# Three of eight convolution tiles on ScalarE and GpSimd with logarithms between filler copies, and the modulation's products on VectorE in the feed-forward

## The chip, the core and the metric

The kernel runs on one NeuronCore of a Trainium2 chip. TensorE (PE) multiplies, VectorE (DVE), ScalarE (ACT) and GpSimd (POOL) work on tiles of 128 partitions, and SyncE (SP) issues the loads of the weights. The metric is the device time of one execution in microseconds; a kernel's time is the median of its runs. All arithmetic is float32.

## The reference, cut to what matters

The whole is a transformer block (two attention mixers, cross-attention to a memory, a feed-forward with a squared ReLU), followed by a second block whose input is modulated by a condition. Three parts of it are touched.

```python
# modulation: a vector times w_ada (1024 x 6144), for the condition c and for c_ctx
mx = silu(c) @ w_ada + b_ada ; mc = silu(c_ctx) @ w_ada + b_ada
xsh1, xsc1, xg1, xsh2, xsc2, xg2 = split(mx, 6)     # only the first two are used of mc
px = (x * (1 + xsc1) + xsh1) @ w_in                 # ctx likewise, with mc
...
# feed-forward of the first block, ahead of it
x = x + square(relu(h @ w_ff_in)) @ w_ff_out        # 1024 -> 4096 -> 1024
...
# convolution branch of the second block, 1024 channels = 8 tiles of 128
u = a * sigmoid(g)                                  # conv_glu, 512 tokens
conv[t] = conv_b + sum_j dw[j] * u[t + j - 15]      # 31 taps for each channel
...
# the decays of the recurrent branch (HGRN), forward and backward
log_f = log(sigmoid(z))  ;  b = cumsum(log_f)       # b and its edges give the weights of keys
```

## The kernel before, in words

The kernel is one program for each engine; semaphores order them (`line.at(name)` is the count at which a named step is done). A generator such as `fill` or `Beside.steps` hands out a program's pieces a few at a time, so that a side job is written between the steps of the main one. The order of the code is the order on the engine. Weights come in panels of 2 MB, through three slots of SBUF in the order of the list `ORDER`: SyncE loads a panel when the panel three places before it has been released (`done`).

The stages in order of time are: norm and projection; the latent stage (`latent_*`), in which VectorE makes rotated queries and keys for four tiles of 128 tokens, `ro(i)`, and TensorE turns them, `T(i)`; the compression (`compress_*`, lines 555 to 672); the first attention; cross-attention; the feed-forward (`ffn_*`); HGRN for the first half of the heads (`hgrn_*` with gq 0), then for the second (gq 1); the merge of the branches; the second attention; and a mixture of experts, half of the span.

**Modulation.** `ada_tensor` (line 437) multiplies the pair of conditions (`SC`, 128 x 2 in each of eight pieces) by twelve panels `w_ada`: eight matmuls of 512 columns for each panel. ScalarE copies each row out (line 467); for panels 0 to 3 TensorE turns the row into columns for `MOD`, for 4 to 11 ScalarE sends it to memory (`ROWD`, semaphores `s_row`). These pieces stand between the steps of the latent stage and of the compression: panels 0 to 7 in the latent stage, 8 ahead of the key matmuls of the compression (line 642), 9 to 11 behind its value matmuls (line 650). The first attention waits for all rows, since the row buffer `RB` lies in its memory. `MOD` is first read in the feed-forward's last part (`modulated_*`).

**Feed-forward.** Eight panels `w_ff_in` give 32 tiles `h`: TensorE multiplies (line 258), ScalarE takes the ReLU (line 1338), VectorE squares (line 1354). Eight panels `w_ff_out` (line 1327) follow.

**HGRN, gq 1.** TensorE makes the projections q (4 tiles), z and zc for two directions (4 and 4 each) and v (6 tiles), all through eight banks of PSUM, and then two panels of filler work, 16 steps of `aside_tensor` (line 1385): projections that later stages need, which go through banks 6 and 7, a copy by ScalarE (line 1399) and a store by GpSimd (line 1409). ScalarE takes sigmoids and copies of the projections. Beside that, VectorE makes the convolution (`taps_vector`): for each of eight tiles k it multiplies the gated input, then does one product with a first tap (line 1467) and 30 of `sum = u * tap + sum` (line 1471) in SBUF. GpSimd loads the tiles (lines 1482, 1483) and stores the sums to memory (line 1487). The logarithms' buffers (`LOGS`) share memory with the tap tiles. So ScalarE first finishes its eight filler copies (`fill(16)`), waits for VectorE's last tap and for the stores (`s_cv`), and then runs the four logarithm jobs (`log_scalar`: absolute value, exponential, logarithm; lines 1500, 1502, 1504); VectorE turns each into cumulative sums (`log_vector`, lines 1515 to 1529), takes the differences to the edges (`decay`, line 1756), ScalarE exponentiates (lines 1685, 1686), VectorE weighs the keys (line 1760), and TensorE, which has been through its filler, turns them (line 1596's loop with its transposes, `kt`) and makes the states.

## Time and profile before

| | us |
|---|---|
| median of 3 runs | 4361.85 |
| lowest and highest of them | 4344.37 and 4363.55 |
| the profiled execution | 4348.94 |
| its span, first to last instruction | 4347.0 |

Busy shares of the span are 83% for TensorE, 50% for VectorE, 19% for ScalarE and 28% for GpSimd. A matmul in float32 is two records; 128 x 512 records follow each other at 0.43 us at the full clock. The rows below are one kind each: a timeline row is the start in us, the length of a run of like instructions, engine, line, operation, output and input, count, and in brackets how long the engine had been idle before and what released it. Times on GpSimd are rough.

### The profile page before, as it was taken

Reading aid. Unit: us, or ns where it says so; the run is one execution under the profiler, and the core shown is the slowest. Engines: PE = TensorE matmul, PEld = TensorE weight load, DVE = VectorE, ACT = ScalarE, POOL = GpSimd, SP = SyncE. Lnnn points to the kernel's source line nnn. Section 1 sums busy time; section 2 is a strip of 40 time slices with the busy share of each in tenths; the row PEclk is TensorE's granted clock in tenths of the full one; section 3 lists DMA queues with packets and bytes.
Section 4 is the critical chain, followed back from the end, with each engine's and each line's share of the span. In section 5 each row is a group of like instructions: output and inputs, shape, how many; then the busy total and the mean of one; then the engine's idle time right before and its main releaser. Section 6 shows DMA issues by size and latency. Waiting matters only on the chain.

```text
span 4347.0 us, 33067 instructions
## 1 busy us (share of the span) xinstructions
PE 3596.0 (83%) x10942; PEld 1813.3 (42%) x10942; DVE 2153.0 (50%) x4711; ACT 845.3 (19%) x1796; POOL 1226.4 (28%) x1151
## 2 busy tenths in 40 slices
PE   8778998999997989939999974668776877776877
PEld 4334554444453564426644563334232333232322
DVE  0547523100013567966525448863686876433442
ACT  1224422000032221132211223011121221111111
POOL 0200000000000000000001013453787777777774
PEclk9876999999999989969999987889898998988988
DMA  3340021222211112200222256774999999999996
GB/s 152 138 150 1 1 97 49 77 77 77 97 58 49 63 54 104 76 34 34 75 76 97 104 196 214 258 248 160 385 338 348 342 365 359 355 370 369 353 377 263
DMA packets 171912, 765.16 MB, mean 176 GB/s; under 512 B 19256, under 2 KB 19256, under 8 KB 160224
## 3 DMA queue, kind: packets, MB, share of 16 engines
q0 software_dynamic: 157904, 580.06, 36.2%
q1 hardware_dynamic: 13824, 182.97, 11.5%
q8 instruction: 89, 1.46, 0.1%
q14 instruction: 79, 0.65, 0.0%
q10 hardware_dynamic: 16, 0.02, 0.0%
HBM read 744.08 MB, written 18.89 MB: 176 GB/s over the span
## 4 chain that ended last, share of the span: by engine, by line
PE 49%; DVE 20%; issue 8%; DMA 5%; POOL 4%; ACT 2%; another core or an unknown queue 1%; POOLq 0%; DVEq 0%; ACTq 0%
PE ps L252 13%; PE ps L258 9%; PE ps L2591 8%; DVE arena L2668 5%; PE ps L1327 5%; PE ps L1385 5%; DVE arena L1471 4%; POOL arena L2638 4%; DMA arena<-in_pu,arena 3%; PE ps L1609 2%; PE ps L220 2%; DMA arena<-in_pv,arena 2%; PE ps L1596 1%; PE ps L831 1%
## 5 line engine op out<-in xcount | busy, mean ns | idle before, releaser
L2591 PE MATMUL ps<-arena 128*128 128x512 f32 x2048 | 1031.1, 655 | 385.0 <-issue 163.9
L2591 PEld LDWEIGHTS ps<-arena 128*128 128x128 f32 x2048 | 404.9, 206 | 991.1 <-issue 786.8
L2668 DVE CUSTOM_DVE_ANT_0 arena<-arena 128x1024 f32<-128x1024 f32 x512 | 622.5, 1221 | 387.8 <-DMA arena<-in_pu,arena 350.2
L252 PE MATMUL ps<-arena 128*128 128x512 f32 (+1 forms) x1768 | 755.0, 587 | 31.5 <-ACT arena L2157 24.4
L2638 POOL DMA_INDIRECT arena<-in_pu,arena x512 | 559.2, 1092 | 419.8 <-issue 96.5
L2638 POOL DMA_INDIRECT arena<-in_pv,arena x512 | 557.5, 1089 | 196.3 <-issue 136.0
L258 PE MATMUL ps<-arena 128*128 128x512 f32 (+2 forms) x1408 | 527.7, 536 | 3.1 <-DVE arena L1300 0.9
L252 PEld LDWEIGHTS ps<-arena 128*128 128x128 f32 x1768 | 337.2, 192 | 434.8 <-issue 429.7
L258 PEld LDWEIGHTS ps<-arena 128*128 128x128 f32 x1408 | 268.2, 191 | 262.8 <-issue 220.4
L220 PE MATMUL ps<-arena 128*128 128x128 f32 (+1 forms) x1062 | 191.4, 314 | 203.0 <-ACT arena L1686 59.8
L263 POOL TENSOR_TENSOR arena<-arena 128x1 f32<-128x1 f32 (+7 forms) x38 | 61.4, 1617 | 1012.6 <-DVE arena L675 427.7
L2607 ACT ACTIVATE arena<-arena 128x128 f32<-128x128 f32 x512 | 191.5, 396 | 760.2 <-PE ps L2591 345.4
L1385 PE MATMUL ps<-arena 128*128 128x512 f32 x640 | 293.0, 605 | 16.6 <-ACT arena L1686 12.8
L220 PEld LDWEIGHTS ps<-arena 128*128 128x128 f32 (+1 forms) x1062 | 138.4, 159 | 291.3 <-issue 100.6
L1327 PE MATMUL ps<-arena 128*128 128x512 f32 x512 | 220.2, 592 | 1.4 <-DVE arena L1354 1.4
L1409 POOL DMA_DIRECT2D aside<-arena x20 | 10.7, 534 | 710.8 <-ACT arena L1399 710.8
L1471 DVE SCALAR_TENSOR_TENSOR arena<-arena 128x512 f32<-128x512 f32 x240 | 180.6, 753 | 8.4
L1385 PEld LDWEIGHTS ps<-arena 128*128 128x128 f32 x640 | 118.6, 193 | 143.7 <-issue 125.5
L1327 PEld LDWEIGHTS ps<-arena 128*128 128x128 f32 x512 | 97.1, 190 | 123.7 <-issue 121.5
L1609 PEld LDWEIGHTS ps<-arena 128*128 128x128 f32 x896 | 119.0, 209 | 31.1 <-issue 17.4
L1283 POOL DMA_DIRECT2D x_spill<-arena x1 | 0.6, 578 | 447.6 <-DVE arena L1351 447.6
L1609 PE MATMUL ps<-arena 128*128 128x64 f32 x896 | 118.2, 289 | 6.2 <-DVE arena L1804 6.1
(334 smaller groups left out, 3120.8 us busy)
## 6 DMA issues: line engine op xcount, KB each, us to landing
arena<-in_w_in SPq DMA_DIRECT2D x27, 2048.0 KB, 9.6
arena<-in_w_ada SPq DMA_DIRECT2D x12, 2048.0 KB, 8.1
arena<-in_w_ff_in SPq DMA_DIRECT2D x8, 2048.0 KB, 7.8
arena<-in_w_ff_out SPq DMA_DIRECT2D x8, 2048.0 KB, 8.1
arena<-in_w_pq SPq DMA_DIRECT2D x8, 2048.0 KB, 8.1
aside<-arena POOLq DMA_DIRECT2D x20, 512.0 KB, 6.8
arena<-in_w_at SPq DMA_DIRECT2D x4, 2048.0 KB, 8.4
arena<-in_w_o SPq DMA_DIRECT2D x4, 2048.0 KB, 8.0
```

The lines of the kernel that those rows point to most:

```text
L220: return t.transpose(ps, src, ID[0:src.shape[0], 0:src.shape[0]])
L252: x = t.matmul(PS[:, b, 0:n], hT[:, k, i * 128:(i + 1) * 128], w[:, k, :], start=k == 0, stop=k == nk - 1)
L258: x = t.matmul(PS[:, b, 0:n], w[:, k, f * 128:(f + 1) * 128], hT[:, k, 0:n], start=k == 0, stop=k == nk - 1)
L263: return g.tensor_tensor(o, o, MH[0:o.shape[0], 0:o.shape[-1]], ALU.pow)
L1327: x = t.matmul(PS[:, 4 * c + i, :], AT[:, 8 * kk + k, 128 * i:128 * i + 128], w[:, k, :], start=kk == 0 and k == 0, stop=kk == 3 and k == 7)
L1385: x = t.matmul(PS[:, b, :], l, r, start=k == 0, stop=k == 7)
L1471: tap.V.own(v).scalar_tensor_tensor(out=cv, in0=u[:, j:j + 512], scalar=dw[:, 8 * j + k:8 * j + k + 1], in1=cv, op0=ALU.mult, op1=ALU.add) ...
L1609: x = t.matmul(PS[:, b, 64 * c:64 * c + 64].rearrange("p (n t) -> p n t", t=w), WL[lv % 4][:, o:o + 128], sides(WL[lv % 4][:, o:o + 128], ...
L2591: x = t.matmul(PS[:, b + c, :], DG[n % 4], row(f)[:, 512 * c:512 * c + 512], start=j == 0, stop=j == 127)
L2607: a.activation(DG[n % 4], ID, ACT.Copy, scale=GS[i][:, j:j + 1]).then_inc(*pe.A.step("dg", n))
L2638: g.indirect_dma_start(PLACES[SPOT[n]], None, d[tab], bass.IndirectOffsetOnAxis(ap=EXU[i][:, j:j + 1], axis=0)).then_inc(s_row_in[SPOT[n]] ...
L2668: v.tensor_tensor_reduce(row(f), row(f), TT[i], 1.0, 0.0, ALU.mult, ALU.add, DOT[i % 2][:, j:j + 1]).then_inc(*pe.V.step("dot", 128 * i + j))
```

## The change

Three things move.

- The `w_ada` panels leave the latent stage and the compression. They now stand in `ORDER` between the panels of the feed-forward, one behind each of the first twelve. For each, VectorE multiplies the eight 512-wide pieces by a column of `SC` and adds them up (two conditions for panels 0 to 3, one for 4 to 11); TensorE adds over the partitions, with 8 small matmuls against a column of ones for panels 0 to 3 and one 512-wide matmul for 4 to 11; ScalarE copies out. The attention no longer waits for `s_row`.
- The convolution of gq 1 is split. VectorE has tiles 0 to 4 and keeps the sums in PSUM (banks 4 and 5, which leaves six for the projections); ScalarE copies each sum out (`move_out`). For tiles 5 to 7 ScalarE makes each product into one of three buffers, and GpSimd adds it to the sum: 93 products, 90 adds.
- The four logarithm jobs stand between the 16 filler steps on ScalarE, where they stood behind all of them.

```diff
-        ORDER = ([("w_in", c) for c in range(4)] + [("w_ada", c) for c in range(9)] + [("w_cmp", 0), ("w_cmp", 1)]
-                 + [("w_ada", c) for c in range(9, 12)] + [("scratch", 0), ("w_xk", 0), ("w_xv", 0), ("w_out", 0), ("w_out", 1),
-                                                           ("w_xq", 0), ("w_xo", 0)]
-                 + [("w_ff_in", c) for c in range(8)] + [("w_ff_out", c) for c in range(8)]
+        FF = [("w_ff_in", c) for c in range(8)] + [("w_ff_out", c) for c in range(8)]
+        ORDER = ([("w_in", c) for c in range(4)] + [("w_cmp", 0), ("w_cmp", 1), ("scratch", 0), ("w_xk", 0), ("w_xv", 0),
+                                                    ("w_out", 0), ("w_out", 1), ("w_xq", 0), ("w_xo", 0)]
+                 + [p for c in range(12) for p in (FF[c], ("w_ada", c))] + FF[12:]
...
+        def ada_sums_tensor(t, c, banks):
+            t.wait_ge(*ad.V.at("acc", c))
+            b = bank(t, banks, ad.A, "row", c)
+            if c < 4:
+                for r in range(2):
+                    for k in range(4):
+                        x = t.matmul(PS[:, b, 8 * r + 2 * k:8 * r + 2 * k + 2], ADA[c % 2][r][:, 128 * k:128 * k + 128], cs("one")[:, 0:2],
+                                     start=True, stop=True)
+            else:
+                x = t.matmul(PS[0:2, b, :], cs("one")[:, 0:2], ADA[c % 2][0], start=True, stop=True)
+            x.then_inc(*ad.P.step("row", c))
+
...
+        def ada_sums_vector(v, c):
+            w = w3("w_ada", c)
+            v.wait_ge(*loaded("w_ada", c))
+            if c > 1:
+                v.wait_ge(*ad.P.at("row", c - 2))
+            for k in range(8):
+                ad.V.own(v)
+                for r in range(ada_conditions(c)):
+                    o, s = ADA[c % 2][r], SC[:, k, r:r + 1]
+                    if k == 0:
+                        v.tensor_scalar(o, w[:, k, :], s, None, ALU.mult).then_inc(*ad.V.step("acc", c))
+                    else:
+                        v.scalar_tensor_tensor(out=o, in0=w[:, k, :], scalar=s, in1=o, op0=ALU.mult, op1=ALU.add
+                                               ).then_inc(*ad.V.step("acc", c))
+            done("w_ada", c, ad.V)
...
                     mm_feat(t, b, HT, 8, w3("w_ff_in", c), a, 512).then_inc(*ff.P.step("h", 4 * c + a))
+                    if c and a == 1:
+                        ada_sums_tensor(t, c - 1, BANKS)
...
+                        if c == 0 and i == 1:
+                            ada_sums_tensor(t, 7 + kk, (4, 5, 6, 7))
+                        if c == 0 and kk == 3 and i == 3:
+                            ada_sums_tensor(t, 11, (4, 5, 6, 7))
...
                 v.tensor_tensor(AT[:, f, :], AT[:, f, :], AT[:, f, :], ALU.mult).then_inc(*ff.V.step("h", f))
+                if f % 4 == 0:
+                    ada_sums_vector(v, f // 4)
+            for c in range(8, 12):
+                ada_sums_vector(v, c)
+            ad.V.own(v)
...
+        s_cv = [sem(f"s_cv{k}") for k in range(8)]
+        s_tap = [sem(f"s_tap{k}") for k in range(5)]
+        TAPU = [A[:, TFo + 1054 * j:TFo + 1054 * j + 542] for j in range(5)]
+        TAPC = [A[:, TFo + 1054 * j + 542:TFo + 1054 * j + 1054] for j in range(5)]
+        TAPP = [A[:, TFo + 5270 + 512 * j:TFo + 5782 + 512 * j] for j in range(3)]
+        ONV, ONG = (0, 1, 2, 3, 4), (5, 6, 7)
+        TAPBANK = (4, 5)
...
+            def move_out(k):
+                a.wait_ge(*tap.V.at("conv", k))
+                a.activation(TAPC[tap_slot(k)], PS[:, TAPBANK[k % 2], :], ACT.Copy).then_inc(*tap.A.step("out", k))
+            for k in (0, 5, 1, 6, 2):
+                gate(k)
+                yield
+            for n, k in enumerate(ONG):
+                u, cv = TAPU[tap_slot(k)], TAPC[tap_slot(k)]
+                a.wait_ge(*tap.V.at("input", k))
+                for j in range(31):
+                    x = u[:, j:j + 512]
+                    if j == 0:
+                        a.activation(cv, x, ACT.Identity, scale=tap_weight(k, 0), bias=pr("cb")[:, k:k + 1]).then_inc(*tap.A.step("product", k, 0))
+                    else:
+                        m = 30 * n + j - 1
+                        if m > 2:
+                            a.wait_ge(*tap.G.at("sum", m - 3))
+                        a.activation(TAPP[m % 3], x, ACT.Copy, scale=tap_weight(k, j)).then_inc(*tap.A.step("product", k, j))
+                    yield
+                    if (n, j) == (0, 20):
+                        move_out(0)
+                    if (n, j) == (1, 7):
+                        move_out(1)
+                    if (n, j) == (1, 14):
+                        gate(3)
+                    if (n, j) == (1, 20):
+                        gate(7)
+                    if (n, j) == (1, 24):
+                        move_out(2)
+                    if (n, j) == (1, 28):
+                        gate(4)
+                    if (n, j) == (2, 11):
+                        move_out(3)
+            move_out(4)
 
         def taps_vector(v):
-            dw = pr("dw")
-            for k in range(8):
-                u, cv = TAPU[k % 6], TAPC[k % 6]
-                if k < 6:
+            def prepare(k, first):
+                u = TAPU[tap_slot(k)]
...
-                v.tensor_tensor(u[:, 15:527], u[:, 15:527], cv, ALU.mult).then_inc(*tap.V.step())
-                tap.V.own(v).tensor_scalar(cv, u[:, 0:512], dw[:, k:k + 1], pr("cb")[:, k:k + 1], ALU.mult, ALU.add
+                v.tensor_tensor(u[:, 15:527], u[:, 15:527], TAPC[tap_slot(k)], ALU.mult).then_inc(*tap.V.step("input", k))
+            for k in ONV:
+                u, sums = TAPU[tap_slot(k)], PS[:, TAPBANK[k % 2], :]
+                prepare(k, k < 3)
+                if k > 1:
+                    v.wait_ge(*tap.A.at("out", k - 2))
+                tap.V.own(v).tensor_scalar(sums, u[:, 0:512], tap_weight(k, 0), pr("cb")[:, k:k + 1], ALU.mult, ALU.add
                                            ).then_inc(*tap.V.step())
                 yield
+                if k in (0, 1, 3):
+                    prepare({0: 5, 1: 6, 3: 7}[k], k < 2)
                 for j in range(1, 31):
-                    tap.V.own(v).scalar_tensor_tensor(out=cv, in0=u[:, j:j + 512], scalar=dw[:, 8 * j + k:8 * j + k + 1], in1=cv,
+                    tap.V.own(v).scalar_tensor_tensor(out=sums, in0=u[:, j:j + 512], scalar=tap_weight(k, j), in1=sums,
                                                       op0=ALU.mult, op1=ALU.add).then_inc(*tap.V.step("conv", k))
                     yield
...
+            def add(n, k, first, last):
+                cv = TAPC[tap_slot(k)]
+                for j in range(first, last):
+                    g.wait_ge(*tap.A.at("product", k, j))
+                    tap.G.own(g).tensor_tensor(cv, cv, TAPP[(30 * n + j - 1) % 3], ALU.add).then_inc(*tap.G.step("sum", 30 * n + j - 1))
+            for k in (0, 5, 1, 6, 2):
+                fetch(k)
+            add(0, 5, 1, 26)
+            g.wait_ge(*tap.A.at("out", 0))
+            put(0)
+            add(0, 5, 26, 31)
+            g.wait_ge(*tap.G.at("sum", 29))
+            put(5)
+            g.wait_ge(s_cv[0], 16)
+            fetch(3)
+            add(1, 6, 1, 8)
+            g.wait_ge(s_cv[5], 16)
+            fetch(7)
+            add(1, 6, 8, 10)
+            g.wait_ge(*tap.A.at("out", 1))
+            put(1)
+            add(1, 6, 10, 18)
+            g.wait_ge(s_cv[1], 16)
+            fetch(4)
+            add(1, 6, 18, 31)
+            g.wait_ge(*tap.G.at("sum", 59))
+            put(6)
+            add(2, 7, 1, 8)
+            g.wait_ge(*tap.A.at("out", 2))
+            put(2)
+            add(2, 7, 8, 16)
+            g.wait_ge(*tap.A.at("out", 3))
+            put(3)
+            add(2, 7, 16, 31)
+            g.wait_ge(*tap.G.at("sum", 89))
+            put(7)
+            g.wait_ge(*tap.A.at("out", 4))
+            put(4)
 
...
+            banks = (0, 1, 2, 3, 6, 7) if gq else BANKS
             t.wait_ge(*loaded("w_in2", gq))
             for f in range(4):
-                b = bank(t, BANKS, st.V, "q", f)
+                b = bank(t, banks, st.V, "q", f)
...
             if gq:
                 fill(16)
+                t.wait_ge(*tap.A.at("out", 4))
```

In `hgrn_scalar`, with the number of side steps for gq 1 behind each q, z, zc and v tile going from 10, 11, 6 and 10 to 6, 6, 3 and 6, the end of the projections is now as follows. `taps_over` waits for VectorE's last tap and for all eight stores; TensorE waits for `move_out(4)` behind its filler.

```diff
+            if gq:
+                beside.work += [taps_over(a)] + [log_scalar(a, st, r) for r in range(4)]
+                for _ in range(16):
+                    fill(1)
+                    beside.steps(6)
             beside.steps(ALLSTEPS)
-            if gq:
-                fill(16)
-                a.wait_ge(*tap.V.end())
-                a.wait_ge(s_cv[0], 16)
-                a.wait_ge(s_cv[1], 16)
-                a.wait_ge(s_cv[2], 96)
-                beside.work += [log_scalar(a, st, r) for r in range(4)]
-                beside.steps(ALLSTEPS)
```

TensorE in the latent stage and the compression, before: L444 is a modulation panel, L252 the projections, L220 transposes, L642 and L650 keys and values, L919 the first scores of the attention.

```order
L220 MATMUL ps<-arena 128x128 x18
L252 MATMUL ps<-arena 128x512 x4
L252 MATMUL ps<-arena 128x128
L444 MATMUL ps<-arena 2x512 x32
L220 MATMUL ps<-arena 128x128 x36
L444 MATMUL ps<-arena 2x512 x8
L642 MATMUL ps<-arena 32x128 x32
L650 MATMUL ps<-arena 128x128 x32
L444 MATMUL ps<-arena 2x512 x24
L220 MATMUL ps<-arena 128x32 x2
L919 MATMUL ps<-arena 128x32 x8
```

After (lines 600, 608 and 874 are the old 642, 650 and 919):

```order
L220 MATMUL ps<-arena 128x128 x18
L252 MATMUL ps<-arena 128x512 x4
L252 MATMUL ps<-arena 128x128
L220 MATMUL ps<-arena 128x128 x36
L600 MATMUL ps<-arena 32x128 x32
L608 MATMUL ps<-arena 128x128 x32
L220 MATMUL ps<-arena 128x32 x2
L874 MATMUL ps<-arena 128x32 x8
```

No panel stands between the transposes any more, none behind the value matmuls. ScalarE in gq 1, from the last v copy to the first exponentials of the decays, before (L1671 v, L1399 filler copies, L1500 to L1504 logarithms):

```order
L1671 ACTIVATE arena<-ps 128x512
L1399 ACTIVATE arena<-ps 128x512 x8
L1500 ACTIVATE arena<-arena 128x1024
L1502 ACT_TABLE_LOAD
L1502 ACTIVATE arena<-arena 128x1024
L1504 ACT_TABLE_LOAD
L1504 ACTIVATE arena<-arena 128x1024
L1500 ACTIVATE arena<-arena 128x2048
L1502 ACT_TABLE_LOAD
L1502 ACTIVATE arena<-arena 128x2048
L1504 ACT_TABLE_LOAD
```

After (L1780 v, L1491 `move_out`, L1420 filler copies, L1601 to L1605 logarithms):

```order
L1491 ACTIVATE arena<-ps 128x512
L1780 ACTIVATE arena<-ps 128x512 x5
L1601 ACTIVATE arena<-arena 128x1024
L1603 ACT_TABLE_LOAD
L1603 ACTIVATE arena<-arena 128x1024
L1605 ACT_TABLE_LOAD
L1605 ACTIVATE arena<-arena 128x1024
L1420 ACTIVATE arena<-ps 128x512
L1601 ACTIVATE arena<-arena 128x2048
L1603 ACT_TABLE_LOAD
L1603 ACTIVATE arena<-arena 128x2048
L1605 ACT_TABLE_LOAD
```

The first logarithm job now stands ahead of all filler copies, the second behind one of them, and the last `move_out` ahead of five of the six v copies. ScalarE beside the z tiles of gq 1, before (L1664 and L1665 are z's sigmoid and copy, L1454 a gate):

```order
L1664 ACTIVATE arena<-ps 128x512
L1665 ACTIVATE arena<-ps 128x512
L1664 ACTIVATE arena<-ps 128x512
L1665 ACTIVATE arena<-ps 128x512
L1454 ACTIVATE arena<-arena 128x512
L1664 ACTIVATE arena<-ps 128x512
```

After (L1773, L1774 z, L1506 products for GpSimd, L1491 `move_out(2)`, L1487 gate):

```order
L1773 ACTIVATE arena<-ps 128x512
L1774 ACTIVATE arena<-ps 128x512
L1506 ACTIVATE arena<-arena 128x512
L1491 ACTIVATE arena<-ps 128x512
L1506 ACTIVATE arena<-arena 128x512 x4
L1487 ACTIVATE arena<-arena 128x512
L1506 ACTIVATE arena<-arena 128x512
L1773 ACTIVATE arena<-ps 128x512
L1774 ACTIVATE arena<-ps 128x512
L1506 ACTIVATE arena<-arena 128x512
```

Each copy of a z tile, which frees TensorE's bank, now has up to six products ahead of it, each product from the fourth on waiting for a GpSimd add.

## Rows read from the trace of the kernel before

**Rows 1.** The page, section 4: the chain that ended last, by engine.

```profile
PE 49%; DVE 20%; issue 8%; DMA 5%; POOL 4%; ACT 2%; another core or an unknown queue 1%; POOLq 0%; DVEq 0%; ACTq 0%
```

**Rows 2.** Timeline of TensorE, HGRN gq 1.

```profile
1652.07 110.27 PE L258 MATMUL ps<-arena 128*128 128x512 f32 x320 [0.73 <-DVE arena L245]
1762.17 41.36 PE L252 MATMUL ps<-arena 128*128 128x512 f32 x96
1803.37 55.10 PE L1385 MATMUL ps<-arena 128*128 128x512 f32 x128
1918.31 0.66 PE L220 MATMUL ps<-arena 128*128 128x128 f32 x2 [59.84 <-ACT arena L1686]
```

**Rows 3.** Timeline of VectorE, the same stage: one tile of taps, first and last of the logarithms.

```profile
1786.43 0.67 DVE L1466 TENSOR_TENSOR arena<-arena 128x512 f32<-128x512 f32 x1
...
1787.72 23.59 DVE L1471 SCALAR_TENSOR_TENSOR arena<-arena 128x512 f32<-128x512 f32 x30
...
1876.63 1.23 DVE L1515 SCALAR_TENSOR_TENSOR arena<-arena 128x1024 f32<-128x1024 f32 x1 [15.65 <-ACT arena L1504]
...
1911.84 2.29 DVE L1529 TENSOR_TENSOR arena<-arena 128x2048 f32<-128x2048 f32 x1
```

**Rows 4.** Timeline of ScalarE, the same stage.

```profile
1840.89 0.60 ACT L1399 ACTIVATE arena<-ps 128x512 f32<-128x512 f32 x1 [9.26 <-DMA aside<-arena]
...
1870.81 1.06 ACT L1500 ACTIVATE arena<-arena 128x1024 f32<-128x1024 f32 x1 [11.71 <-DMA conv<-arena]
...
1896.87 1.91 ACT L1504 ACTIVATE arena<-arena 128x2048 f32<-128x2048 f32 x1
...
1915.64 0.21 ACT L1685 ACTIVATE arena<-arena 128x8 f32<-128x8 f32 x1 [15.56 <-DVE arena L1756]
...
1926.55 0.36 ACT L1693 ACTIVATE arena<-ps 128x256 f32<-128x256 f32 x1
```

**Rows 5.** GpSimd's groups with shapes kept apart: busy, mean ns of one.

```profile
L263 POOL TENSOR_TENSOR arena<-arena 128x30 f32<-128x30 f32 x4 | 24.5, 6122 | 59.1 <-DVE arena L560 43.4 <-DVE arena L549 15.7
...
L1487 POOL DMA_DIRECT2D conv<-arena x8 | 4.3, 544 | 119.7 <-DVE arena L1464 119.5 <-DVE arena L1471 0.3
...
L378 POOL CAST lmask<-arena 128x1920 uint8<-128x1920 f32 x1 | 1.8, 1784 | 44.9 <-DMA arena<-in_lm 44.9
```

**Rows 6.** Timeline of VectorE, latent stage and compression.

```profile
174.36 2.16 DVE L547 TENSOR_TENSOR arena<-arena 128x1920 f32<-128x1920 f32 x1 [13.79 <-ACT arena L523]
...
199.75 2.16 DVE L547 TENSOR_TENSOR arena<-arena 128x1920 f32<-128x1920 f32 x1 [9.05 <-ACT arena L523]
...
227.74 0.96 DVE L576 TENSOR_TENSOR arena<-arena 128x768 f32<-128x768 f32 x1 [5.28 <-PE ps L220]
...
240.00 0.97 DVE L598 TENSOR_TENSOR arena<-arena 128x496 f32<-128x496 f32 x1
...
258.97 1.98 DVE L610 COPY arena<-ps 32x64 f32<-32x64 f32 x8 [14.03 <-PE ps L650]
...
286.11 0.49 DVE L987 TENSOR_TENSOR arena<-ps,arena 128x128 f32<-128x128 f32 x2 [21.42 <-DMA ada_rows<-arena]
```

**Rows 7.** Timeline of TensorE, latent stage and compression.

```profile
197.95 27.63 PE L444 MATMUL ps<-arena 128*2 128x512 f32 x64
...
244.44 7.15 PE L642 MATMUL ps<-arena 128*32 128x128 f32 x64
...
258.86 20.76 PE L444 MATMUL ps<-arena 128*2 128x512 f32 x48
```

**Rows 8.** Windows: stretch, its length, busy time (instructions) of PE, PEld, DVE, ACT, POOL, then granted clock, DMA share, GB/s.

```profile
120.00:128.00 8.00, 3.08 (x15) 3.12 (x16) 4.20 (x16) 2.58 (x5) 3.00 (x3) 0.50 0.32 137
...
737.60:957.30 219.70, 219.70 (x510) 96.93 (x508) 21.54 (x31) 18.51 (x31) 0.00 (x0) 1.00 0.20 72
```

**Rows 9.** Timeline of TensorE: 16 records with narrow moving data.

```profile
2001.75 1.90 PE L1609 MATMUL ps<-arena 128*128 128x64 f32 x16
```

**Rows 10.** The page, section 6: loads of the modulation's panels, KB each, median us to landing.

```profile
arena<-in_w_ada SPq DMA_DIRECT2D x12, 2048.0 KB, 8.1
```

166 lines of the change are left out of this document (70 added, 96 removed).

## The prediction

> **What bounds the kernel now.** I read the chain that ended last first: TensorE has 49% of it, VectorE 20% [rows 1]. So what counts is where TensorE stands still, and what extra work it gets where it doesn't. Two places are touched in which it waits or does work that could lie elsewhere, and one in which it has no gap.
>
> The first place is HGRN gq 1. TensorE's projections run from 1652.07 to 1803.5, its filler to 1858.5, and then it is idle for 59.84 us until 1918.31 [rows 2]. Meanwhile VectorE makes eight tiles of taps, one in 1786.43 to 1811.31, 24.9 us [rows 3]. ScalarE waits for the last store until 1870.81, makes the logarithms until 1898.8, and waits for VectorE until 1915.64 [rows 4]. VectorE's sums over the logarithms take 1876.63 to 1914.13, 37.5 us [rows 3].
>
> The second is the latent stage and the compression, where the modulation's panels lie partly in TensorE's waits for VectorE and partly in the way. In the third, the feed-forward, TensorE is busy for all of 219.7 us at the full clock, and VectorE for 21.5 us [rows 8].
>
> **Part 1, the panels leave the early stages.**
> - VectorE waited 13.79 us for the gather of tile 2, where the same wait for tile 3 was 9.05 [rows 6]; the difference of 4.7 is panels' copies on ScalarE. It waited 5.28 us for T(2), which stood behind panels 4 to 7 (27.63 us) [rows 6, 7]. Both go: 10.0.
> - The keys' input was ready at 240.0 [rows 6], their matmuls began at 244.44 behind panel 8 [rows 7]: 4.4.
> - Panels 9 to 11 take 20.76 us [rows 7], where VectorE's chain from 258.97 (8 copies in 1.98 us [rows 6], then some fifteen small steps of 0.2 to 0.3 us) takes about 6: 14.8.
> - The first attention step on VectorE began at 286.11, released by the last row's store [rows 6]. Panels ended at 279.6, and some 3 us of transposes, copies and first scores follow. So about 3.5 were the store's.
>
> That is 32.7 us. Against it: TensorE now idles for most of the latent stage, and in gaps it falls to 1.2 GHz: 0.50 granted at 120 to 128 us, when it had waited for VectorE [rows 8]. The transposes, the projections and the key matmuls (7.15 us at full clock [rows 7]) lie on the path and could take up to twice as long where they begin cold. I take off 8: four transposes at 2 us more. Bounds are 33 (never cold) and 10 (all of it cold). **Minus 25.**
>
> **Part 2, the panels in the feed-forward.** TensorE gets, for panels 0 to 3, 8 matmuls of 128 x 2, 16 records each. Nearest are 16 narrow records in 1.90 us [rows 9]: 7.6. For 4 to 11 it gets one 512-wide matmul each, two records at 27.63 / 64 = 0.43 [rows 7]: 6.9. All of it is on the path, since TensorE has no gap there. Is anything late? A feed-forward panel lasts 219.7 / 8 = 27.5 us [rows 8]. Panel c of the modulation can be loaded when w_ff_in c - 1 is released, and lands 8.1 us later [rows 10]. VectorE's 16 steps at 0.79 us (23.59 / 30 [rows 3]) are 12.6, so the sum is there 21 us into the panel, and TensorE asks for it at 27.5 + 14. The last one (panel 11) is ready after 8.1 + 6.3 = 14.4 us and asked for at 21. The next w_ff_in panel is issued right behind the modulation's and lands at 16. VectorE's squares queue behind the wait for a panel, but only the last of them is waited for, and panel 7 is done by then. ScalarE's small copies free only the banks of the sums. So nothing else is paid, and **plus 14.5**; bounds 13 and 25 (a start-up of a us for each of 12 insertions).
>
> **Part 3, the convolution and the logarithms.** There are three chains in 1652 to 1803.
> - VectorE: 5 tiles at 24.9 are 124.4, 3 more inputs of 0.7, and q's. From 1660.7 it ends at about 1790. No row shows a sum written to PSUM. With the 0.79 us of the SBUF sums it ends at 1790, with 1.0 at 1822.
> - GpSimd: 90 adds of 128 x 512. No add of this size is in the trace. The cast of 1920 columns takes 1.784 us [rows 5], 0.93 ns a column, so one input of 512 would be 0.48 us. The power on 30 columns takes 6.1 us [rows 5], which is an iterated function and no near neighbour. I take two inputs at the cast's rate, 0.95, and 0.35 for the start and two semaphores, 1.3 us. It starts at about 1667, behind gates and first products. With 14 DMA issues of 0.54 [rows 5] it ends at 1667 + 117 + 8 = 1792.
> - ScalarE follows GpSimd by three buffers. TensorE, with six banks, needs the copy of the third z tile of direction 1 by 1762, when v begins [rows 2]. Ahead of it are 65 adds and about 6 us of issues, so it is in time while an add takes up to 1.37 us. Each 0.1 us more costs 6.5 us.
>
> The Trainium skill, GPSIMD Engine Reference, "3.1 Elementwise — side-by-side cycle accounting", gives 4497 ns for a two-input float32 add of 2048 columns, about twice VectorE's. An estimate from it for 512 columns is 1.1 us, and by it part 3 comes out as below. It speaks against such adds in general. The Trainium skill, SBUF — State Buffer, "Who interferes with whom", says that a VectorE instruction with two SBUF inputs contends with a GpSimd instruction that reads SBUF. No row here shows it; with the sums in PSUM only the eight gated inputs are of that kind.
>
> The last `move_out` stands ahead of five v copies. It waits for 1790, and v's last tile ends at 1803.5, so the banks hold. The stores are issued at about 1798; the last one before took until 1870.81 [rows 4], 9 us, so it may be 1807 when the logarithms start. Job 0 and one filler copy take until 1814, job 1 about 8 us, job 2 5 and job 3 8: ScalarE is through at about 1837, since all four took 28 us before [rows 4]. TensorE has two filler banks and stands still for some 5 us in that time, as ScalarE comes late to a filler copy. VectorE's last sums (14 us of the 37.5) then end at about 1852, while the filler copies end at about 1864 instead of 1859. Then the first exponential of the decays comes at about 1865, where it came at 1915.64 [rows 4]; what follows is unchanged, its first copy of turned keys again 10.9 us later [rows 4]. **Minus 51.** Bounds: 56 with no late filler copy, 35 with an add of 1.6 us.
>
> **Sum.** -25 + 14.5 - 51 = -61.5. Against the profiled execution's 4348.94 (span 4347.0 and 1.9 around it) that is 4287. The median shown is 12.9 above that execution, and the runs spread by 19. I take half of the 12.9: **4294**.
>
> **The rivals.**
> 1. *An add takes 1.4 to 2.2 us.* ScalarE comes late to z and v, TensorE stalls for banks, and the gain shrinks: at 1.7 by 0.33 x 65 = 21, 4315; at 2.2 by 54, 4348. For it: two inputs, each with a wait for the engine's own last result. Against it: the cast's rate. Chance 0.15.
> 2. *A sum in PSUM takes about 1.0 us on VectorE.* It ends at 1822, `move_out(4)` holds five v copies until then, and TensorE's filler starts some 20 us late: 4314. Chance 0.08.
> 3. *Slower than before.* One mechanism: GpSimd's add is of the power's kind, and all of z, v, filler and logarithms queue behind it on ScalarE. The whole gain of 61.5 is gone at 1.37 + 61.5 / 65 = 2.3 us, half a percent is lost at 2.65; at 3.0 it is 4400. For it: GpSimd's only other arithmetic in the trace is very slow [rows 5]. Against it: an add isn't iterated. Chance 0.07.
> 4. *The overlap doesn't come, though the taps are early:* the logarithms on ScalarE and the filler hold each other up (two banks, one staging buffer whose store once made ScalarE wait 9.26 us [rows 4]) so that TensorE loses 25 instead of 5 us: 4314. Chance 0.08.
>
> The forecast has 0.62.
>
> **How the numbers follow.** The forecast's own range is 4270 to 4310 (part 1 by +15 or -8, part 3 by +16 or -5, the runs' spread). To hold 8 in 10 it must take in rivals 2, 4 and most of 1: 4262 to 4342. Half a percent (22 us) is about what a measurement can tell from no change; below 4340 lie the forecast, rivals 2 and 4 and most of 1: 0.88. Within it are the rest of 1 and a little of 3: 0.06. Slower: 0.06.
>
> **What would show it.** After the change, the wait of 59.84 us should be gone and the first exponential should come about 12 us behind the end of TensorE's filler at most; an add should be near 1.1 us, with products on ScalarE waiting for GpSimd; a PSUM sum should be near 0.79. In the feed-forward TensorE should be busy throughout and 14 us longer, with no wait for VectorE. The attention should begin 25 us earlier, with a lower granted clock ahead of it. I am wrong if TensorE waits for banks in z or v, or if ScalarE's row of filler copies ends later than 1870 on the old scale.

## The result and the profile after

The changed kernel takes 4294.35 us (median of 4, 4277.35 to 4303.53), the kernel before on the same chip 4353.11 (median of 4, 4335.31 to 4363.55). The ratio is 0.987, with a 95% interval of 0.984 to 0.990: 1.3% faster, 58.8 us by the medians. The forecast was 4294.

One execution of each kernel was profiled. The one after is the fastest of its four (4277.35, span 4275.5), so the spans differ by 71.5 us, 13 more than the medians. Up to the first matmul of the mixing stage behind HGRN (where the branches are merged) the profiles differ by 50.25 us, and a second profile of the changed kernel gives 53.3 there; the other 21 us lie behind it, and I come back to them below.

The timeline of TensorE in the changed kernel, start and duration first, the wait ahead of it in brackets: the first attention transposes, the output stage, the first matmuls of the feed-forward, the first sum of a modulation panel, the first HGRN group.

```profile
262.60 0.66 PE L220 MATMUL ps<-arena 128*128 128x128 f32 x2 [4.82 <-DVE arena L955]
...
547.01 27.70 PE L252 MATMUL ps<-arena 128*128 128x512 f32 x64 [2.22 <-DMA arena<-in_w_out]
...
712.56 43.67 PE L258 MATMUL ps<-arena 128*128 128x512 f32 x96 [0.78 <-DVE arena L1134]
756.07 1.84 PE L1265 MATMUL ps<-arena 128*128 128x2 f32 x16
...
1180.33 19.98 PE L258 MATMUL ps<-arena 128*128 128x512 f32 x46 [0.92 <-DVE arena L1253]
```

The same four places in the kernel before:

```profile
291.09 0.66 PE L220 MATMUL ps<-arena 128*128 128x128 f32 x2 [8.53 <-DVE arena L1000]
...
571.32 27.70 PE L252 MATMUL ps<-arena 128*128 128x512 f32 x64 [0.71 <-DMA arena<-in_w_out]
...
735.12 5.13 PE L258 MATMUL ps<-arena 128*128 128x512 f32 x6 [0.79 <-DVE arena L1183]
...
1186.64 13.54 PE L258 MATMUL ps<-arena 128*128 128x512 f32 x31 [0.92 <-DVE arena L1300]
```

So 28.5 us are won at the attention, 22.6 are left at the feed-forward, 6.3 behind it.

TensorE in the second HGRN group of the changed kernel, the same view as [rows 2]:

```profile
1643.21 110.27 PE L258 MATMUL ps<-arena 128*128 128x512 f32 x320 [0.73 <-ACT arena L236]
1753.31 41.36 PE L252 MATMUL ps<-arena 128*128 128x512 f32 x96
1794.51 27.63 PE L1406 MATMUL ps<-arena 128*128 128x512 f32 x64
1825.54 29.40 PE L1406 MATMUL ps<-arena 128*128 128x512 f32 x64 [3.40 <-ACT arena L1420]
1859.56 0.66 PE L220 MATMUL ps<-arena 128*128 128x128 f32 x2 [4.62 <-DVE arena L1864]
1867.99 1.19 PE L1699 MATMUL ps<-arena 128*128 128x128 f32 x4 [7.76 <-ACT arena L1799]
```

The projections are as long as before (110.27 and 41.36 us): no bank was late. The wait of 59.84 us of [rows 2] is gone; 3.40 in the middle of the filler and 4.62 behind it are left. From the group's start to the first turned keys it was 266.24 us and is 216.35.

ScalarE in the same place: the first logarithm job, a late filler copy, the last filler copy, the first exponential of the decays, the first copy of turned keys (compare [rows 4]).

```profile
1795.21 1.05 ACT L1601 ACTIVATE arena<-arena 128x1024 f32<-128x1024 f32 x1
...
1824.82 1.07 ACT L1420 ACTIVATE arena<-ps 128x512 f32<-128x512 f32 x2
...
1854.98 0.60 ACT L1420 ACTIVATE arena<-ps 128x512 f32<-128x512 f32 x1 [6.21 <-PE ps L1406]
...
1856.89 0.21 ACT L1791 ACTIVATE arena<-arena 128x8 f32<-128x8 f32 x1
...
1867.48 0.36 ACT L1799 ACTIVATE arena<-ps 128x256 f32<-128x256 f32 x1
```

The costliest groups from 1643 to 1860: after the bar the busy time and the mean ns of one, then the idle time before them. They are VectorE's sums in PSUM, GpSimd's additions and ScalarE's products.

```profile
L1543 DVE SCALAR_TENSOR_TENSOR ps<-arena,ps 128x512 f32<-128x512 f32 x150 | 113.4, 756 | 5.2
...
L1563 POOL TENSOR_TENSOR arena<-arena 128x512 f32<-128x512 f32 x90 | 105.6, 1173 | 22.6 <-ACT arena L1506 10.6 <-POOL arena L1563 0.4
L1506 ACT ACTIVATE arena<-arena 128x512 f32<-128x512 f32 x90 | 65.0, 726 | 39.8 <-POOL arena L1563 39.3
```

And the additions alone, min, median and max ns, first and last start:

```profile
L1563 POOL TENSOR_TENSOR arena<-arena x90: 1082/1091/1709, 1659.6 to 1783.1; 128x512 f32<-128x512 f32 x90
```

From first to last start a step takes 123.5 / 89 = 1.39 us. ScalarE waited 39.3 us for GpSimd, GpSimd 10.6 for ScalarE, nearly all of them ahead of its first addition, so GpSimd sets the pace of these three tiles. They end at 1784, VectorE's five at 1781.6: the split is even.

### The profile page after: what moved, and what is told of

Same layout as the page of the kernel before. It is cut to its first block, busy times and chain, and to the rows that moved or that the text cites. A ratio compares the mean times of both kernels' runs of the same rounds, so it can differ in the third digit from the quotient of the medians.

```text
span 4275.5 us, 33127 instructions
## 1 busy us (share of the span) xinstructions
PE 3543.1 (83%) x10814; PEld 1818.0 (43%) x10814; DVE 2175.2 (51%) x4744; ACT 910.9 (21%) x1890; POOL 1332.9 (31%) x1241
## 4 chain that ended last, share of the span: by engine, by line
PE 51%; DVE 15%; issue 9%; POOL 6%; DMA 4%; ACT 3%; another core or an unknown queue 1%; POOLq 0%; DVEq 0%; ACTq 0%
PE ps L252 14%; PE ps L258 12%; POOL arena L2742 6%; PE ps L1406 6%; DVE arena L2772 5%; PE ps L1336 5%; PE ps L2695 5%; DMA arena<-in_pu,arena 3%; PE ps L1712 2%; PE ps L220 2%; DMA arena<-in_pv,arena 1%; PE ps L1699 1%; PE ps L786 1%; PE ps L2320 1%
## 5 line engine op out<-in xcount | busy, mean ns | idle before, releaser
L2695 PEld LDWEIGHTS ps<-arena 128*128 128x128 f32 x2048 | 400.3, 205 | 974.2 <-issue 765.6
L252 PE MATMUL ps<-arena 128*128 128x512 f32 (+1 forms) x1768 | 757.7, 589 | 33.2 <-ACT arena L2261 24.4
L252 PEld LDWEIGHTS ps<-arena 128*128 128x128 f32 x1768 | 338.4, 193 | 438.3 <-issue 433.6
L258 PEld LDWEIGHTS ps<-arena 128*128 128x128 f32 x1408 | 267.2, 190 | 261.1 <-issue 216.9
L220 PE MATMUL ps<-arena 128*128 128x128 f32 x1046 | 198.8, 327 | 199.0 <-ACT arena L812 49.8
L220 PEld LDWEIGHTS ps<-arena 128*128 128x128 f32 x1046 | 144.9, 166 | 282.1 <-issue 136.0
L1406 PEld LDWEIGHTS ps<-arena 128*128 128x128 f32 x640 | 118.6, 194 | 147.7 <-issue 129.4
L1336 PEld LDWEIGHTS ps<-arena 128*128 128x128 f32 x512 | 96.7, 190 | 125.7 <-issue 123.4
L1712 PEld LDWEIGHTS ps<-arena 128*128 128x128 f32 x896 | 119.1, 209 | 30.9 <-issue 16.7
L1543 DVE SCALAR_TENSOR_TENSOR ps<-arena,ps 128x512 f32<-128x512 f32 x150 | 113.4, 756 | 5.2
## 6 DMA issues: line engine op xcount, KB each, us to landing
arena<-in_w_ff_out SPq DMA_DIRECT2D x8, 2048.0 KB, 12.4
```

Source lines behind the costliest of these rows:

```text
L220: return t.transpose(ps, src, ID[0:src.shape[0], 0:src.shape[0]])
L252: x = t.matmul(PS[:, b, 0:n], hT[:, k, i * 128:(i + 1) * 128], w[:, k, :], start=k == 0, stop=k == nk - 1)
L258: x = t.matmul(PS[:, b, 0:n], w[:, k, f * 128:(f + 1) * 128], hT[:, k, 0:n], start=k == 0, stop=k == nk - 1)
L1336: x = t.matmul(PS[:, 4 * c + i, :], AT[:, 8 * kk + k, 128 * i:128 * i + 128], w[:, k, :], start=kk == 0 and k == 0, stop=kk == 3 and k == 7)
L1406: x = t.matmul(PS[:, b, :], l, r, start=k == 0, stop=k == 7)
L1543: tap.V.own(v).scalar_tensor_tensor(out=sums, in0=u[:, j:j + 512], scalar=tap_weight(k, j), in1=sums, op0=ALU.mult, op1=ALU.add).then_inc( ...
```

## Experiments

Three questions: do the two parts add up, which piece of the large one brings the gain, and where did some of it go again. The kernel before had a median of 4363.8 us beside the first four kernels, 4353.2 beside the next four and 4363.7 beside the last, so kernels are compared by their ratios to it.

### One part alone

The modulation's part alone; nothing of the convolution or the logarithms is touched:

```diff
-                 + [("w_ff_in", c) for c in range(8)] + [("w_ff_out", c) for c in range(8)]
+                 + [p for c in range(12) for p in (FF[c], ("w_ada", c))] + FF[12:]
...
+                    if c and a == 1:
+                        ada_sums_tensor(t, c - 1, BANKS)
```

> The modulation's move alone; convolution and logarithms as in the kernel before. My theory: the first attention transposes come 28 us earlier (about 262.6), the feed-forward starts 22 us earlier and lasts 16 us longer, so the first HGRN group starts 6 us earlier (1180) and the time is 6 us below the kernel before (4347, 4341 to 4350), with the last stretch (from the first matmul of the mixing stage to the end) about as long as in the kernel before. Rival: the profile of the changed kernel ended 71.5 us earlier though its mixing stage began only 50 us earlier, and the 21 us come with the order of the panels; then this kernel is 27 us faster than before (4326) and its last stretch is 20 us shorter.

Measured: 4358.17 against 4363.78, ratio 0.9988 (0.9969 to 1.0007), 5.6 us less. Attention at 261.95, feed-forward at 711.76, first HGRN group at 1179.56, second at 1642.47. The interval takes in no change at all, so the part's worth is read from the profile and not from the times. The starts are those of my theory; the rival (27 us) fell, and the span behind the first mixing matmul is 2175.1, as in the kernel before (2175.9). But of the 9.6 us by which the second group starts earlier nothing is left at its end: the first mixing matmul comes at 2171.32, in the kernel before at 2171.13. The wait ahead of the keys was 0.9 us longer and the rest of the group 8.9, at 1.2 GHz, of which more below.

The other part alone: three tiles on ScalarE and GpSimd, logarithms between filler copies.

```diff
+        ONV, ONG = (0, 1, 2, 3, 4), (5, 6, 7)
...
+                for _ in range(16):
+                    fill(1)
+                    beside.steps(6)
```

> The three convolution tiles on ScalarE and GpSimd and the logarithms between the filler copies alone; modulation as in the kernel before. My theory: from the start of the second HGRN group to its first key transposes 216.3 us instead of 266.2 (50 less), of which 8 are lost in the rest of the group since TensorE stays at 1.2 GHz longer, so 41 to 44 us below the kernel before (4311, 4305 to 4317). Rival that the last stretch is shorter because of this part: 4288 to 4291. Together the two parts should add up: the sum of the two differences is that of the changed kernel within 5 us.

Measured: 4319.48, ratio 0.9892 (0.986 to 0.9923), 44.3 us less. In its profile the first turned keys come at 1868.18, 216.33 us behind the group's start at 1651.85. The last stretch was 2192.7 us, so the rival fell too. The two ratios together, 0.9988 and 0.9892, make 0.988, the changed kernel's 0.987 within the intervals. In microseconds the two gains are 49.9 together, and the changed kernel's is 58.8, or 51.2 in its second measurement: my 5 us are missed against the one and met against the other, and the intervals allow both.

### The logarithms behind the filler

```diff
-                for _ in range(16):
-                    fill(1)
-                    beside.steps(6)
+                fill(16)
             beside.steps(ALLSTEPS)
```

> The changed kernel with all sixteen filler copies of ScalarE first and the logarithms after them, instead of six steps of the logarithms behind each copy. If the interleaving is what hides the logarithms, the last filler copy comes at about 1850 and the first key transposes some 40 us after it, at 1893 to 1897 instead of 1859.6, and the time is 30 to 38 us above the changed kernel (4324 to 4332). If the logarithms were hidden by the split of the convolution alone (VectorE and ScalarE free earlier), the time stays within 5 us of the changed kernel (4294). If keeping TensorE cold for longer costs as well, the rest of the group is longer by up to 8 us more.

Measured: 4342.45, ratio 0.9948 (0.9928 to 0.9967); the changed kernel has 0.9867, so 35 us are lost, as expected if the interleaving hides the logarithms. TensorE and ScalarE in this kernel:

```profile
1793.49 55.10 PE L1406 MATMUL ps<-arena 128*128 128x512 f32 x128
1896.76 0.66 PE L220 MATMUL ps<-arena 128*128 128x128 f32 x2 [48.18 <-ACT arena L1790]
```

```profile
1848.62 0.60 ACT L1420 ACTIVATE arena<-ps 128x512 f32<-128x512 f32 x1 [6.21 <-PE ps L1406]
1849.12 1.05 ACT L1601 ACTIVATE arena<-arena 128x1024 f32<-128x1024 f32 x1
```

The first logarithm comes right behind the last filler copy, and the wait of 48.18 us is there again. The convolution is split as in the changed kernel, and from the group's start to the keys it is 254.6 us. So of the 49.9 us that the part wins there, the split alone brings 11.7 (266.2 to 254.6) and the interleaving the other 38.2. By the code the split is what makes the interleaving possible, since the logarithms may start only when the taps have left their memory; the interleaving without the split wasn't run. The expectation that the rest of the group would be longer by up to 8 us was wrong: it was 4 us shorter than in the changed kernel.

### The sums of VectorE in SBUF

```diff
-                u, sums = TAPU[tap_slot(k)], PS[:, TAPBANK[k % 2], :]
+                u, sums = TAPU[tap_slot(k)], TAPC[tap_slot(k)]
```

ScalarE's `move_out` stays and copies the tile in SBUF onto itself, so that nothing else in the order of the work changes.

> The changed kernel with VectorE's running sums of its five tiles in SBUF in place of PSUM, so that its 150 operations read two SBUF tiles each while GpSimd adds. Theory 1 (the two engines do not hinder each other): VectorE's operation 0.79 us instead of 0.756, its end 5 us later (1786), GpSimd's adds as before (mean 1.17 us, last near 1783), time 4294 to 4299. Theory 2 (VectorE with two SBUF inputs and GpSimd hold each other up, as the Trainium skill's page SBUF - State Buffer, section Who interferes with whom, says): the adds' mean rises to 1.5 us or more and their pitch above 1.7, the last add after 1810, and the time is 25 us or more above the changed kernel (over 4319). With the sums in PSUM the adds had a pitch of 1.24 us alone and about 1.42 beside VectorE's sums, so a part of theory 2 might be seen in the changed kernel already.

Measured: 4361.07, ratio 1.0003 (0.9984 to 1.0022). The whole gain is gone; against the changed kernel it is 59 us slower. VectorE's sums (four records are missing) and GpSimd's additions in this kernel, min, median and max ns:

```profile
L1543 DVE SCALAR_TENSOR_TENSOR arena<-arena x146: 747/1465/2414, 1654.4 to 1847.5; 128x512 f32<-128x512 f32 x146
```

```profile
L1563 POOL TENSOR_TENSOR arena<-arena x90: 1102/1357/1642, 1656.9 to 1838.5; 128x512 f32<-128x512 f32 x90
```

The timelines show the two in step, ScalarE's products with them. GpSimd and VectorE early in the stage:

```profile
1660.58 7.46 DVE L1543 SCALAR_TENSOR_TENSOR arena<-arena 128x512 f32<-128x512 f32 x5
...
1661.63 7.36 POOL L1563 TENSOR_TENSOR arena<-arena 128x512 f32<-128x512 f32 x5
```

One sum of VectorE takes 1.5 us (7.46 for 5) where it took 0.79 in [rows 3] with no addition on GpSimd, and 0.79 with the sums in PSUM (23.71 us for 30 in the changed kernel). Theory 2 holds, but by another road than I expected: the additions' mean is 1.40 us, not 1.5 (1.17 in the changed kernel), and the larger loss is VectorE's, whose 150 sums have a mean of 1.23 us instead of 0.756: 71 us more busy time, where GpSimd has 20 more. ScalarE then waits for it before it can copy a finished tile out, and comes late to z and v, and TensorE stands still for a bank. ScalarE's copy of a finished tile, and TensorE's longest wait:

```profile
1770.43 0.63 ACT L1491 ACTIVATE arena<-arena 128x512 f32<-128x512 f32 x1 [15.11 <-DVE arena L1543]
```

```profile
1776.83 6.71 PE L258 MATMUL ps<-arena 128*128 128x256 f32 x16 [16.57 <-ACT arena L1774]
```

By the Trainium skill, SBUF — State Buffer, "Who interferes with whom", a VectorE instruction with two SBUF inputs contends with a GpSimd one that reads SBUF. The trace agrees: 1.5 us for VectorE's sum beside the additions against 0.79 without them.

### A dearer addition

A second addition whose result nothing uses goes ahead of each, of 512 or of 160 columns. GpSimd also waits once, ahead of the first, until an earlier store from the scratch tile `STG` is through (not shown in the cut):

```diff
                     g.wait_ge(*tap.A.at("product", k, j))
+                    p = TAPP[(30 * n + j - 1) % 3][:, 0:512]
+                    tap.G.own(g).tensor_tensor(STG[:, 0:512], p, p, ALU.add).then_inc(*tap.G.step())
```

> The changed kernel with a second GpSimd addition of 512 columns, whose result nothing uses, ahead of each of the 90, so that a step of the chain of products and sums costs about 2.35 us instead of 1.24 to 1.42. By the prediction's third rival (an addition twice or three times as dear turns the gain into a loss; break-even at 2.3) the last sum comes some 90 to 100 us later (1875 to 1885), logarithms and filler copies behind it, the first key transposes at 1940 to 1955, and the time is 80 to 95 us above the changed kernel, 20 to 35 above the kernel before. If other work sets the end there and the additions have slack, less than 50 us above the changed kernel.

> The same with a second addition of 160 columns only (0.4 us by its share of 1.09 for 512, and what one instruction costs whatever its size). The prediction gave 6.5 us for each 0.1 us of an addition beyond 1.37 us. The chain had a mean of 1.37 us a step in the changed kernel, so 0.4 us more is 36 us of chain; the end is then 26 to 36 us above the changed kernel (4320 to 4330 where that has 4294). If the step is nearer 1.24 and the product on ScalarE fills the rest, 20 us or less.

Measured: 4388.92 against 4353.23 with 512 columns, ratio 1.0077 (1.0047 to 1.0107), and 4328.43 with 160, ratio 0.9944 (0.9923 to 0.9965). Against the changed kernel's second measurement (4302.07, below) that is 86.9 and 26.4 us more, both as expected, the second at its lower end. The useful additions in the first, then in the second:

```profile
L1565 POOL TENSOR_TENSOR arena<-arena x90: 1081/1093/1602, 1659.2 to 1881.5; 128x512 f32<-128x512 f32 x90
```

```profile
L1565 POOL TENSOR_TENSOR arena<-arena x90: 1082/1092/1566, 1656.9 to 1827.2; 128x512 f32<-128x512 f32 x90
```

A step takes 222.3 / 89 = 2.50 and 170.3 / 89 = 1.91 us instead of 1.39. From the group's start to the turned keys it is 308.5 and 261.4 us instead of 216.3: 92.1 and 45.1 more, 8.3 and 8.6 for each 0.1 us of a step. That fits the 90 steps that stand ahead of the logarithms (9.0) better than the 65 ahead of the last z copy (6.5). TensorE does stand still for the copies of z and v as the prediction's rival had it, up to this wait in the kernel with 512 columns:

```profile
1724.66 9.78 PE L258 MATMUL ps<-arena 128*128 128x512 f32 x16 [11.21 <-ACT arena L1777]
```

The line between the two measured times (24.8 us below the kernel before at 1.91, 35.7 above it at 2.50) crosses it at a step of 2.15 us.

### The changed kernel again, and TensorE kept busy

> The changed kernel itself once more, beside the two kernels below on one chip. If the part of its profile that no theory of mine explains is the spread of single executions, two things differ from its first profile: the last stretch (first matmul of the mixing stage to the end; 2154.6 us there, 2175.9 in the kernel before, 2173 to 2193 in four kernels with the same code there) comes out nearer 2175, and the point at which TensorE returns to 2.4 GHz in the second HGRN group (51 us after the first key transposes there, 30 in the kernel before) may move. If they are the change's doing, both repeat within 3 us. The ratio to the kernel before stays at 0.987, plus or minus 0.002.

Measured: 4302.07 against 4353.23, ratio 0.9872 (0.9846 to 0.9898). The last stretch, from the first mixing matmul at 2117.86 to the end at 4302.7, was 2184.8 us; it was 2154.6 in this kernel's first profile. Over the ten profiles of the changed kernel and of those made for the experiments, all with the same code there, it lies between 2154.6 and 2196.2. So the 21 us belong to the spread of single executions. The second thing that I had called a possible spread did repeat: from the first keys to the mixing stage it was 261.32 and 261.30 us. By my own expectation that speaks for the change; the windows below say how far.

The next kernel puts extra matmuls, whose result is overwritten, into the waits of 4.62 and 7.76 us around the first keys:

```diff
+                        b = bank(t, (0, 1, 2, 3), st.A, "kt", part, dr, 0)
+                        warm(t, b, 8)
                     t.wait_ge(*st.V.at("kd", part, dr))
...
+                            warm(t, b, 16)
                         t.wait_ge(*st.A.at("kt", part, dr, h))
```

> The changed kernel with 24 additional matmuls of 512 columns whose results are overwritten: 8 in TensorE's 4.6 us wait before the first key transposes of the second HGRN group, 16 in the 7.8 us wait behind them. They take 0.43 us each at 1.2 GHz, 3.4 and 6.9 us, so they fit and delay nothing by more than 1 us. Theory: the group loses some 9 to 15 us because TensorE runs at 1.2 GHz for 51 us after its first key transposes; kept busy it returns to 2.4 GHz sooner, the rest of the group takes 249 to 253 us instead of 261.3, and the time is 8 to 12 us below the changed kernel. Rival: the gaps of 0.6 to 0.8 us between the small matmuls keep it at 1.2 GHz whatever stood ahead; then the time is that of the changed kernel within 3 us.

Measured: 4291.47, ratio 0.9859 (0.9833 to 0.9886). The intervals overlap with the changed kernel's; the profile is clearer. TensorE's timeline (L1654 are the additional matmuls):

```profile
1852.16 7.03 PE L1654 MATMUL ps<-arena 128*128 128x512 f32 x16
1859.03 0.38 PE L220 MATMUL ps<-arena 128*128 128x128 f32 x2
1859.25 13.90 PE L1654 MATMUL ps<-arena 128*128 128x512 f32 x32
1872.98 0.61 PE L1710 MATMUL ps<-arena 128*128 128x128 f32 x4
```

A matmul of 512 columns is two records of 0.43 us at 2.4 GHz, the level at which these ran (7.03 us for 16 records): I had counted one at 1.2 GHz. So they overran both waits, by 2.1 and 5.5 us, and still the group was 7.0 us shorter (470.65 to the mixing stage; 477.64 in the changed kernel's second profile). The rest of the group took 252.2 us, as my theory had it, and the rival fell: the gaps of 0.6 to 0.8 us are still there and the clock stayed up. With 5 and 8 of them:

```diff
-                        warm(t, b, 8)
+                        warm(t, b, 5)
...
-                            warm(t, b, 16)
+                            warm(t, b, 8)
```

> The kernel with additional matmuls again, but 5 and 8 of them instead of 8 and 16. In the profile of the 8 and 16 each matmul of 512 columns was two records of 0.43 us, 0.87 us in all, so they took 7.0 us in a wait of 4.6 and 13.9 in a wait of 7.8: they delayed the keys by 2.1 and then 5.5 us, and of the 15 us that the clock gave back 7 were left. With 5 and 8 they take 4.35 and 6.95 us and fit. Theory: TensorE stays at 2.4 GHz as well, the second HGRN group lasts 463 us from its start to the mixing stage (470.65 with 8 and 16, 477.6 in the changed kernel), and the time is 12 to 16 us below the changed kernel, ratio to the kernel before 0.984. Rival: the shorter stretch of work isn't enough to hold the clock; then TensorE is at 1.2 GHz again behind the keys and the group lasts 475 us or more.

Measured: 4289.26 against 4363.69, ratio 0.9831 (0.9807 to 0.9855). From the group's start at 1642.04 to the mixing stage at 2102.84 it is 460.8 us, 16.8 less than in the changed kernel and somewhat better than the 463 expected; the time is 1.7% below the kernel before. Against the changed kernel it is 0.4% by the ratios, whose intervals overlap by 0.001 to 0.002, and 16.8 us by single profiles. The first 45 us behind the first turned keys of the kernel before, of the modulation's part alone, of the changed kernel, and of the ones with 8 and 16 and with 5 and 8; the third number from the end is the granted clock:

```profile
1918.31:1963.31 45.00, 26.73 (x139) 21.76 (x140) 22.88 (x44) 11.76 (x20) 0.00 (x0) 0.67 0.00 0
```

```profile
1909.61:1954.61 45.00, 28.56 (x112) 23.32 (x112) 20.80 (x38) 10.44 (x18) 0.00 (x0) 0.50 0.00 0
```

```profile
1859.56:1904.56 45.00, 28.60 (x113) 23.40 (x113) 20.48 (x38) 10.59 (x18) 0.00 (x0) 0.50 0.09 32
```

```profile
1859.03:1904.03 45.00, 33.61 (x178) 22.66 (x177) 21.49 (x45) 11.76 (x20) 0.00 (x0) 1.00 0.04 17
```

```profile
1858.17:1903.17 45.00, 31.33 (x175) 21.58 (x176) 29.01 (x56) 13.88 (x22) 0.00 (x0) 1.00 0.09 33
```

The first two kernels have the same code in this group, and TensorE had waited some 60 us in both. Yet one came back to 2.4 GHz within the 45 us and the other stayed at 1.2 (0.50). From the keys to the mixing stage it was 252.8 us in the one and 261.7 in the other. So a late return needs no change of the code. Read in windows of 2 us, the granted clock was back at 1.00 about 29 us after the keys in the kernel before and 52 in the modulation's part alone; in the six profiles in which the keys follow a wait of 4.62 us (two of them of the changed kernel) it took 41 once, 52 three times (among them both of the changed kernel) and 59 twice. With the logarithms behind the filler it took 41. Whether the change makes the late return more frequent stays open. Where the waits ahead of the keys were filled, the clock was 1.00 for all of the first 80 us behind the keys in both, and the rest of the group was shorter, at 252.2 and 244.7 us, than in any of the nine other profiles (252.8 to 261.7).

## Why the prediction was right, point by point

The time was met (4294.35 against 4294.0). Up to the mixing stage the profiles differ by 50.25 us, where the steps gave 61.5. The 11.25 are 2.4 in part 1, 1.8 in part 2, 1.1 in part 3 and 8.5 in the rest of the second HGRN group, less 2.6 by which the first group was shorter (462.9 instead of 465.4, not foreseen; it comes with the modulation's part, 462.9 with that part alone and 465.5 with the other alone, and its cause stays open). In the second profile the difference is 53.3. The medians of four runs each gave 58.8, those of the second measurement 51.2, and runs of one kernel spread by 26 to 28. So the steps together promised 8 to 11 us more than the profiles show up to that point, each by itself is right to some us, and that the time agrees to the last one is luck.

- **Part 1, forecast minus 25.** At the first attention transposes it was minus 28.5, and minus 31.0 in the second profile: the itemised 32.7 nearly in full. The clock did fall there as forecast (0.62 granted from 148 to 233 us, where it was 0.94), but it cost at most 4.2 and 1.7 us on the path in the two profiles, and not 8. Behind it, however, the attention took 284.4 us to the output stage instead of 280.2, and that stage 165.6 instead of 163.8. In all nine profiles with this part the first is 283.6 to 284.7; the second is 165.3 to 165.6 in eight of them and 167.2 in one. At the feed-forward's start, 22.6 are left, 25.3 in the second profile. So 6 us were lost in stages that the forecast held to be unchanged, and its total came near because the 8 taken off for the clock were too many: two errors that partly cancel. 1.5 of the 6 are TensorE's wait for the first panel of `w_out` (2.22 us, where it was 0.71), for which the forecast has no term. The rest is spread over small operations, and which ones wasn't tested.
- **Part 2, forecast plus 14.5.** From the feed-forward's start to the first HGRN group it was 451.5 us and is 467.8, plus 16.3, all TensorE: it is busy for 464.65 of the 467.77 us (448.38 of 451.52 before), at a granted clock of 1.00. Start to start the narrow insertions take 1.70 us each and the 512-wide ones 0.95, 14.4 in all, which is the forecast; the other 1.9 lie in the records of the weights beside them, and their cause wasn't tested. No wait of TensorE for a panel's sum is in it, as forecast. VectorE's operation on a panel takes 0.75 us.

```profile
712.56:1180.33 467.77, 464.65 (x1153) 207.50 (x1153) 121.31 (x178) 29.74 (x52) 1.35 (x2) 1.00 0.32 126
```

- **Part 3, forecast minus 51.** Minus 49.9 from the group's start to the keys. Its steps, moved by the 8.9 us by which the group starts earlier: VectorE's taps to end at 1781, they end at 1781.6; GpSimd's at 1783, 1784; logarithms from 1798, from 1795.2; last filler copy 1855, 1854.98; first exponential 1856, 1856.9; filler stall 5, 3.4.
- **The addition.** Estimated at 1.3 us with its start and two semaphores. It is 1.09 by itself (median), and a step is 1.39 on average. So the estimate was good enough, but it lay close to the bound of 1.37 that I had set: TensorE had no stall at 1.39, and the bound was a little too strict. The estimate from the Trainium skill's GPSIMD Engine Reference, "3.1 Elementwise — side-by-side cycle accounting" (1.1 us for 512 columns), agrees with the median of 1.09.
- **Rival 1 and rival 3** priced a dearer addition at 6.5 us for each 0.1. The runs gave 8.3 to 8.6 in the profile, and a turning point at a step of 2.15 us instead of 2.3: ScalarE's late copies and TensorE's waits for them are as foreseen, but the price of 8.3 to 8.6 is nearer the 90 steps that stand ahead of the logarithms than the 65. Rival 3's condition fell, and its ground with it: the power's 6.1 us for 30 columns say nothing of an addition, which took 1.09 for 512. That the power is slow because it is iterated no run shows; the trace of before has it growing with the columns, from 1.01 us for 4 to 6.12 for 30.
- **Rival 2** (a dearer sum in PSUM) fell: 0.79 us from sum to sum (23.71 / 30). The conflict in SBUF that the prediction named, and for which it gave no price, is the one that counts: there the same sums take 1.5 beside GpSimd.
- **Rival 4** fell: 3.4 us of stall instead of 25.
- **What I left out.** I said that what follows the first turned keys is unchanged. In the first pair of profiles 8.5 us were lost there, at 1.2 GHz. The modulation's part alone shows that this happens with the code of before as well; that it came again in the second profile of the changed kernel leaves open how often. The median after lies 17 us above the profiled execution (4294.35 and 4277.35), so the half of 12.9 us added for such a distance had the right sign and says no more.

## What to carry to other kernels

When work is moved from a full engine to two idle ones, price the whole step between them (result, semaphore, next instruction), count every step ahead of the next stage, and see where the operands lie: here the same operation with its sums in PSUM or in SBUF made the difference between 1.3% and nothing. Splitting the work won 12 us, and what it let start in the shadow of other work 38. A short wait of TensorE ahead of a row of small matmuls can be worth filling, if the filling fits: 11.5 us of matmuls without use, in waits of 12.4, brought 16.8 in one profile against another.

## What the runs showed of the hardware

- VectorE and GpSimd, each with two float32 inputs of 512 columns in SBUF, ran in step at 1.5 us an operation (7.46 and 7.36 us for five). VectorE takes 0.79 with no addition beside it or with its sums in PSUM, and GpSimd's addition 1.09 beside those.
- The steps of GpSimd's chain took 1.25 us in the first tile (31.23 for 25 additions, the first row) and about 1.4 in the second (6.95 for 5, the second), with VectorE's sums in PSUM both times. What the difference comes from stays open.

```profile
1659.59 31.23 POOL L1563 TENSOR_TENSOR arena<-arena 128x512 f32<-128x512 f32 x25 [10.56 <-ACT arena L1506]
...
1713.85 6.95 POOL L1563 TENSOR_TENSOR arena<-arena 128x512 f32<-128x512 f32 x5
```

- Through a row of small matmuls with gaps of 0.6 to 0.8 us TensorE's return from 1.2 to 2.4 GHz took 29 us in one execution and 52 in another with the same code there (the kernel before and the modulation's part alone), which made 252.8 us or 261.7 of the same stretch. With 11.5 or 20.9 us of additional matmuls around the first the granted clock was 1.00 for all of the next 80 us, in two kernels.
- Single executions of one kernel differed by up to 30 us (4350.35 to 4380.24 for the kernel before beside the last), and in the two profiles of the changed kernel what differed lay behind HGRN: 2154.6 and 2184.8 us for the same code.
